# Latent mixer: the threshold search settled by GpSimd instead of VectorE

## The reference, cut to what matters

```python
def dsa_core(k, v, ki, k_pos, topk, q, qi, wi, q_pos):          # mixer A
    sc = jnp.einsum('bqhd,bsd->bqhs', qi, ki).astype(jnp.float32)
    idx_score = jnp.einsum('bqhs,bqh->bqs', jax.nn.relu(sc), wi.astype(jnp.float32))
    idx_score = jnp.where(chunk_mask(q_pos, k_pos)[None], idx_score, -jnp.inf)
    _, sel = lax.top_k(idx_score, topk)
    ...
def mla_core(k_nope, k_rope, v, k_pos, q_nope, q_rope, q_pos):  # mixer B
    logits = (jnp.einsum('bqhd,bshd->bhqs', q_nope, k_nope)
              + jnp.einsum('bqhd,bsd->bhqs', q_rope, k_rope)).astype(jnp.float32)
    logits = logits * (B_NOPE + B_ROPE) ** -0.5
    logits = jnp.where(chunk_mask(q_pos, k_pos)[None, None], logits, -jnp.inf)
    p = jax.nn.softmax(logits, axis=-1).astype(v.dtype)
    out = jnp.einsum('bhqs,bshd->bqhd', p, v)
```

## Time and profile before

| | us |
|---|---|
| median of 3 runs (3003.99 to 3009.82) | 3007.67 |
| profiled execution, its own time | 3008.22 |
| its span on the core | 3006.4 |

### The profile page before, as it was taken

One profiled execution on the slowest core, in us unless ns is written; L12 is line 12 of the kernel. 1 busy time (PEld: TensorE's weight loads), 2 busy tenths in 40 slices (PEclk: granted clock), 3 DMA queues, 4 the chain that ended last, 5 costly groups with the idle time before them and its releaser, 6 DMA issues. The chain is left out here.

```text
span 3006.4 us, 49479 instructions
## 1 busy us (share of the span) xinstructions
PE 2833.9 (94%) x18462; PEld 2368.9 (79%) x18462; DVE 2018.3 (67%) x3648; ACT 1412.2 (47%) x2850; POOL 532.4 (18%) x410
## 2 busy tenths in 40 slices
PE   8986997999999999899999899999899999999998
PEld 6762564668899999788799566865688999998787
DVE  5447999865867776677631565139857777767777
ACT  5335996552444344433243455348724444444333
POOL 0000222420011110465000231000000111114551
PEclk9996999999999999999999999999999999999999
DMA  4111001021233323654411201120112333326442
GB/s 154 46 36 29 14 14 50 2 65 67 75 97 104 107 97 96 235 172 129 168 51 46 92 2 53 56 77 2 58 74 61 101 109 99 104 91 227 154 130 103
DMA packets 203120, 259.04 MB, mean 86 GB/s; under 512 B 27100, under 2 KB 132180, under 8 KB 202900
## 3 DMA queue, kind: packets, MB, share of 16 engines
q1 hardware_dynamic: 202900, 256.10, 25.8%
HBM read 177.90 MB, written 77.64 MB: 85 GB/s over the span
## 5 line engine op out<-in xcount | busy, mean ns | idle before, releaser
L247 PE MATMUL X<-up_th,high 128*128 128x272 f32 x1232 | 356.4, 289 | 4.1 <-ACT up_U L2287 2.9
L249 PE MATMUL X<-up_th,low_r 128*128 128x272 f32 x1232 | 355.2, 288 | 0.0
L247 PEld LDWEIGHTS X<-up_th,high 128*128 128x128 f32 x1232 | 232.2, 188 | 8.3 <-ACT up_U L2287 6.1
L2248 POOL TENSOR_TENSOR up_sum<-up_U 128x512 f32<-128x512 f32 x20 | 33.4, 1669 | 1131.9 <-DVE up_U L2399 1131.9
L249 PEld LDWEIGHTS X<-up_th,low_r 128*128 128x128 f32 x1232 | 231.9, 188 | 0.0
L2381 DVE SCALAR_TENSOR_TENSOR up_cv<-up_G,tap,up_cv 128x1024 f32<-128x1024 f32 (+1 forms) x176 | 130.3, 782 | 136.9 <-ACT up_cv L2296 135.3
L247 PE MATMUL up_x<-up_th,up_high 128*128 128x272 f32 x704 | 202.9, 288 | 1.4 <-DVE up_low_r L1859 1.4
L249 PE MATMUL up_x<-up_th,up_low_r 128*128 128x272 f32 x704 | 203.7, 289 | 0.0
L248 PE MATMUL X<-sums_r,high 128*128 128x272 f32 x528 | 152.0, 288 | 0.0
L247 PE MATMUL up_y<-up_th,up_high 128*128 128x272 f32 x528 | 151.9, 288 | 0.0
L249 PE MATMUL up_y<-up_th,up_low_r 128*128 128x272 f32 x528 | 151.6, 287 | 0.0
(11 more groups left out here) (581 smaller groups left out, 8665.6 us busy)
## 6 DMA issues: line engine op xcount, KB each, us to landing
scratch_a<-up_U SPq DMA_DIRECT2D x44, 544.0 KB, 2.7
low<-in_w_up_dram SPq DMA_DIRECT2D x44, 512.0 KB, 5.1
up_low<-in_w_up_dram SPq DMA_DIRECT2D x44, 512.0 KB, 4.9
scratch_s<-up_sum SPq DMA_DIRECT2D x80, 256.0 KB, 2.0
b_f<-in_w_down_dram SPq DMA_DIRECT2D x40, 512.0 KB, 4.4
a_lo_p_f<-scratch_s SPq DMA_DIRECT2D x40, 512.0 KB, 4.2
a_lo_p_f<-scratch_a SPq DMA_DIRECT2D x30, 512.0 KB, 4.5
scratch_att<-out_x SPq DMA_DIRECT2D x16, 512.0 KB, 2.6
```

Of the source, the lines that this page charges most:

```text
L247: nc.tensor.matmul(out, lh, rh, start=first, stop=False, skip_group_check=on_top)
L249: return nc.tensor.matmul(out, ll, rh, start=False, stop=last, skip_group_check=on_top)
L2248: g.tensor_tensor(t0, a21, a22, ALU.add).then_inc(pair_summed, 1)
```

## The change

Each step is settled on POOL. `settle` leaves DVE's queue and is called at the end of POOL's loop over the units, behind the scaling of unit i's two heads. It waits there for the counts of DVE and ACT. In place of a comparison, a predicated copy and an exclusive or, it takes the sign of `limit - cnt` as 0 or 1, multiplies it with the signed power of two in the new tensor `flip`, adds that to `bits`, halves `flip`, and adds the two into `cand`: five instructions and a sixth for the next candidate, 128x6 each. The first step (step 0) sets `bits` and `flip` from the sign, with five instructions. DVE waits once, at the end of the search, for the last of these. Nothing else of the kernel changes.

```diff
@@ attention: tensors and semaphores @@
+            flip = sb("flip", [P, n_top], mybir.dt.int32)
-            settled, cand_ready = sem("settled"), sem("cand_ready")
+            settled, cand_ready, flipped = sem("settled"), sem("cand_ready"), sem("flipped")
@@ attention: block.gpsimd @@
+            def settle(step):
+                for by, n in (("dve", BY_DVE), ("act", n_top - BY_DVE)):
+                    pool.wait_ge(counted[by], FROM + n * (step + 1))
+                room = top["ok"][:].bitcast(F32)
+                g.tensor_tensor(room, top["limit"][:], top["cnt"][:], ALU.subtract).then_inc(settled, 1)
+                pool.wait_ge(settled, FROM + 4 * step + 1)
+                if step:
+                    g.tensor_scalar(top["cand"][:], room, 0.0, None, ALU.is_ge).then_inc(settled, 1)
+                    pool.wait_ge(settled, FROM + 4 * step + 2)
+                    g.tensor_tensor(top["cand"][:], top["cand"][:], flip[:], ALU.mult).then_inc(settled, 1)
+                    pool.wait_ge(settled, FROM + 4 * step + 3)
+                    g.tensor_tensor(top["bits"][:], top["bits"][:], top["cand"][:], ALU.add).then_inc(settled, 1)
+                    if step + 1 < STEPS:
+                        g.tensor_scalar(flip[:], flip[:], 0.5, None, ALU.mult).then_inc(flipped, 1)
+                else:
+                    g.tensor_scalar(top["bits"][:], room, 0.0, 1.0, ALU.is_ge, ALU.subtract).then_inc(settled, 2)
+                    g.tensor_scalar(flip[:], room, 0.0, 2.0, ALU.is_ge, ALU.mult).then_inc(settled, 1)
+                    pool.wait_ge(settled, FROM + 4)
+                    g.tensor_scalar(flip[:], flip[:], 1.0, float(1 << 30), ALU.subtract, ALU.mult).then_inc(flipped, 1)
+                if step + 1 < STEPS:
+                    pool.wait_ge(settled, FROM + 4 * step + 4)
+                    pool.wait_ge(flipped, FROM + step + 1)
+                    g.tensor_tensor(top["cand"][:], top["bits"][:], flip[:], ALU.add).then_inc(cand_ready, 1)
             for i, (p, t) in enumerate(order):
                 ...
                     g.tensor_scalar(pr, pr, rr[0:n, c:c + 1], 1.0, ALU.mult, ALU.mult).then_inc(prob_ready[h], 1)
+                for step in (SEARCH_AT[i] if mla else ()):
+                    settle(step)
@@ attention: block.vector @@
-            def settle(step):
-                for by, n in (("dve", BY_DVE), ("act", n_top - BY_DVE)):
-                    dve.wait_ge(counted[by], FROM + n * (step + 1))
-                v_.tensor_tensor(top["ok"][:], top["cnt"][:], top["limit"][:], ALU.is_le).then_inc(settled, 1)
-                dve.wait_ge(settled, FROM + 2 * step + 1)
-                if step:
-                    v_.copy_predicated(top["bits"][:], top["ok"][:], top["cand"][:]).then_inc(settled, 1)
-                else:
-                    v_.tensor_scalar(top["bits"][:], top["ok"][:], 1.0, None, ALU.subtract).then_inc(settled, 1)
-                dve.wait_ge(settled, FROM + 2 * step + 2)
-                if step + 1 < STEPS:
-                    v_.tensor_scalar(top["cand"][:], top["bits"][:], 1 << (30 - step), None, ALU.bitwise_xor).then_inc(cand_ready, 1)
                 ...
-                if mla and len(SEARCH_AT[i]) > 1:
-                    settle(SEARCH_AT[i][0])
                 ...
-                if mla and SEARCH_AT[i]:
-                    settle(SEARCH_AT[i][-1])
                 if mla and i == SEARCH_ENDS + 1:
+                    dve.wait_ge(settled, FROM + 4 * STEPS)
                     next_float()
```

## The result

| | before | after |
|---|---|---|
| median, us | 3008.07 (4 runs) | 3204.1 (4 runs, 3199.75 to 3204.33) |
| profiled execution, us | 3008.22 | 3204.28 |
| its span, us | 3006.4 | 3202.5 |
| ratio to before | | 1.065, 95% interval 1.0632 to 1.0669 |

The change makes the kernel 196 us slower; 3210 was forecast, with a range of 3140 to 3285.

A forecast was written before the change was run, and what follows sets the result against it. The prediction took ACT, busy 99% of the search, as the bound, with DVE and PE close behind. 3008.2 us plus 163 for the loop through POOL's queue plus 39 for PE's clock gave 3210 us, range 3140 to 3285.

The forecast's parts named there:

- the loop through POOL's queue: In the search, settle, scaling, transposes, scores, maxima or copies, and counts wait in a ring once per unit: 5.4 us more each.
- last count to the next scaling: On POOL, settle's six dependent instructions with handovers take 2.1 us from the last count (1.1 to 3.7).
- nine units, with the clock's part: In the search, nine units take 98.8 us against 49.9, plus 1.3 us per unit for PE's lowered clock.
- loop at full clock: Term for the search: thirty units, each 5.4 us longer without any loss of PE's clock, add 163 us.
- the clock: On PE in the search, each unit starts at a lowered clock after idling: 1.3 us per unit, +39 us.
- DVE's relief: In the search, DVE loses 25.5 us of busy time, worth nothing while ACT is the bound.
- cross-check of 2.0 us by twice DVE's time: On POOL, six settle instructions at twice DVE's 0.17 us each would take 2.0 us.
- The first settle of the two units with two steps: On POOL, it lies beside ACT's copies and exponential: costed at nothing, or 2 x 2.1 us if those don't cover it.
- the signs named beforehand: Expected in the profile after: longer search, POOL and PE waits, ACT half busy, clock 0.65 to 0.88, other stages unchanged.
- Full clock: Rival: the search closes to a loop, but PE's gaps don't lower its clock; 3171 us (3141 to 3219), chance 0.2.
- low throughout: Rival: in the search loop PE's clock stays low, 3.4 us per unit; 3272 us (3242 to 3320), chance 0.21.
- not slower: Rival: POOL's lead in the search survives; 3007 us, or 2978 if ACT's busy time hides waits; chance 0.04.

The follow-up runs named there:

- spin22: The changed kernel with 22 idle matmuls on PE in each gap in which it waits for POOL: 3154.6 us, ratio 1.0477.
- late: The changed kernel with the settle of unit i behind the scaling of unit i+1 in POOL's queue, not in front: 3017.6 us, ratio 1.0034.
- wait_only: The kernel before, with POOL made to wait for both counts at each unit's end and no instruction added on POOL: 3147.5 us, ratio 1.0463.

## Why the prediction was right

| step | predicted | measured |
|---|---|---|
| the loop through POOL's queue | closes once per unit | it does: 139 us by the wait alone, 187 us back with the settle one unit later |
| last count to the next scaling | 2.1 us (1.1 to 3.7) | 403.24 to 404.95: 1.7 us |
| nine units, with the clock's part | 98.8 + 9 x 1.3 = 110.5 us | 338.08 to 447.14 (starts of the settles of steps 2 and 11): 109.1 us |
| loop at full clock | +163 us | +146.5 us (spin22) |
| the clock | +39 us | +49.5 us (after against spin22) |
| sum | +202 us | +196 us |
| DVE's relief | nothing | nothing |

**The mechanism was right, and read from two places**: from the order of POOL's queue in the code, and from the row that showed how far the scaling ran ahead. The row of 2.2 us of waiting for POOL told that POOL wasn't on the path then. It did not tell what POOL could afford: a lead of 3.2 us became a lag.

**Two terms were mis-sized, and the errors cancel in part.** The settle was put 0.4 us too long: the two-input instructions took 0.20 us and the one-input ones 0.24, near the 0.2 and 0.27 drawn from the larger shapes, but a handover from one to the next took up to 0.16 us and mostly 0.08, not 0.1 to 0.2. The 0.21 us on which the prediction leaned was misread: the number in brackets is how long POOL had been idle before the instruction, not the delay after its releaser, which was 0.09 us there (DVE's reciprocal ended at 352.53). Thirty times 0.4 is 12 of the 16.5 us by which the loop at full clock was overestimated; the other 4 or 5 are not traced and lie within the uncertainty of the ratios. The prediction's cross-check of 2.0 us by twice DVE's time came near by chance: POOL's two-input instructions took 0.20 us, 1.2 times DVE's 0.166 and not twice, and 0.4 of the 1.7 us are handovers. The first settle of the two units with two steps, put at nothing, was not free: the turns that hold it took 13.3 and 13.7 us (from 500.55 and from 609.46) where the turn of the same tile with one step took 11.8 (from 391.50), 3.3 us in both. The clock's part was some 10 us too small. I took 1.3 us per unit from one idle gap and its 3.4 us at the low level; the turn shown above has it for 6.8 us by the same sum ((0.35 + 0.50 + 0.50 + 0.35) x 2 / 0.5), some 1 us of that before PE resumed, and all the scores of the unit fall into it. That the sum came within 6 us of the measured time is partly luck.

**Of the signs named beforehand** the profile shows all: the stretch at 355 us (330 to 380), POOL's wait for the counts at 268.9 us (over 150), PE's for POOL at 150.3 (over 100), ACT busy 49% of the stretch, a clock of 0.73 (0.65 to 0.88), later stages shifted, but for the 8 us in which the last turn ends. In the turn shown PE idles, the clock drops and the unit starts slow; with the gap filled the clock stayed up at 0.99 and 49.5 us came back. The Trainium skill, TensorE: Matmul & The Clock Gate, Part 1 (HAM oscillation), describes such a loop, and the trace agrees.

**The rivals.** "Full clock" falls by the 0.73, "low throughout" by the turns in which the clock came back (to 1.00 between 412 and 418 us, behind the turn shown), and "not slower" by PE's 150 us of waiting. What the prediction didn't see is a smaller thing: even out of the loop, POOL's 1.7 us to the next candidate cost 10 us against DVE's three instructions. Of DVE's 17.2 us of waiting for it in `late`, 6.9 are three waits behind the narrowest maxima (128 keys), where DVE comes to its next count early, and 6.2 are two waits of 3.1 us in the units with two steps, where the next count follows with no maximum between.

## What to carry to other kernels

Before work is moved to an idle engine, write down its queue in order and ask who waits for what stands behind the moved instruction: a wait on the end of a pipeline turn, put ahead of the start of the next turn, closes the pipeline to a loop, whatever the engine's busy share. Price the loop by the whole turn, not by the instructions moved, and count what the idle gap does to TensorE's clock. If such work has to stand there, put it behind the next turn's work in the queue, and keep what follows the wait as short as it can be.

## What the runs showed of the hardware

- A GpSimd instruction on 128x6 elements took 0.195 to 0.20 us with two inputs and 0.235 to 0.245 us with one, with floats and 32-bit integers alike, and a chain of six, each waiting for the one before, 1.77 us. DVE's comparison of the same size took 0.166 us.
- Filling PE's gaps with matmuls that no one reads made the changed kernel 49.5 us faster (granted clock 0.73 to 0.99); filling half of each gap gave 19.5 us (0.88).
- In `wait_only` DVE's small settle instructions fell together with POOL's scaling (427.18 to 428.43 beside 427.04 to 428.40 us in one turn), and the same exclusive or took 0.62 us on average where it took 0.41 before. In that turn the exclusive or ended 0.03 us after POOL's scaling, and so did the longest of the kernel before (0.90 us, 341.57 against 341.54). What holds it up isn't tested.
